# Gate and up projections fed a joined high/low input, later sums of the stick-breaking attention in fp32r for a pair of heads, the second norm's sum behind the first feed-forward block, and the last product in token halves

## What is computed

```
u = rmsnorm(h); q, k, v, u_pool, u_conv = split(u @ w_in)
merged = [rmsnorm(stick_breaking(q,k,v)), rmsnorm(pool(u_pool)), rmsnorm(conv(u_conv))]
h = h + rmsnorm(merged @ w_out)
u = rmsnorm(h); h = h + rmsnorm((silu(u @ w_gate) * (u @ w_up)) @ w_down)
```

## Time and profile before

| | |
|---|---|
| Median of 3 runs | 1150.9 us (1150.71 to 1151.04) |
| The profiled execution | 1150.66 us, span 1148.7 us |
| TensorE busy | 1132.2 us (99% of the span), 8383 matmuls |
| VectorE, ScalarE, GpSimd busy | 672.1, 527.7, 32.2 us |
| HBM traffic | 200.39 MB by DMA, mean 174 GB/s |

### The profile page before, as it was taken

How to read it: one execution, slowest core, us unless ns; L and a number is a source line. 1 busy time by engine, 2 the same in 40 slices (tenths; PEclk the granted TensorE clock), 3 DMA queues, 4 the chain that set the end, 5 groups by cost and what they waited for, 6 DMA issues and landing times.

```text
span 1148.7 us, 21345 instructions
## 1 busy us (share of the span) xinstructions
PE 1132.2 (99%) x8383; PEld 1075.2 (94%) x8383; DVE 672.1 (59%) x787; ACT 527.7 (46%) x642; POOL 32.2 (3%) x45
## 2 busy tenths in 40 slices
PE   9999999999999989999999999999999999999996
PEld 8999999999999989999999999999999888888885
DVE  5599985545556875555556555655565544444543
ACT  6644465755555563433433343334333434343431
POOL 2000101000000220000000000000000000000000
PEclk9999999999999999999999999999999999999999
DMA  7555544434455366665666666565656555555552
GB/s 248 173 168 172 175 129 147 137 115 136 130 181 179 99 200 185 184 186 181 191 188 183 181 184 183 182 187 181 194 172 197 186 199 188 199 188 196 189 195 91
DMA packets 173647, 200.39 MB, mean 174 GB/s; under 512 B 6257, under 2 KB 149825, under 8 KB 173201
## 3 DMA queue, kind: packets, MB, share of 16 engines
q1 hardware_dynamic: 172848, 197.30, 54.7%
q0 software_dynamic: 608, 1.41, 0.4%
q10 hardware_dynamic: 144, 1.05, 0.3%
HBM read 197.63 MB, written 2.10 MB: 174 GB/s over the span
## 4 chain that ended last, share of the span: by engine, by line
PE 96%; DVE 2%; ACT 0%; issue 0%; POOL 0%; POOLq 0%; DVEq 0%; ACTq 0%
PE ps L960 23%; PE ps L962 23%; PE ps L963 23%; PE ps L1280 7%; PE ps L1279 7%; PE ps L1278 7%; PE ps L991 1%; PE ps L1086 1%; PE ps L1074 1%; DVE u L762 1%; DVE arena L875 1%; PE ps L1103 1%; PE ps L1154 1%; DVE xT L882 0%; PE ps L1011 0%
## 5 line engine op out<-in xcount | busy, mean ns | idle before, releaser
L691 DVE TENSOR_TENSOR w_lo<-raw,w_hi 128x1024 fp32r<-128x1024 f32 x368 | 451.8, 1230 | 427.8 <-ACT w_hi L419 427.4
L419 ACT ACTIVATE w_hi<-raw 128x1024 fp32r<-128x1024 f32 x368 | 389.0, 1058 | 500.8 <-PE ps L963 367.2
L960 PE MATMUL ps<-u,w_hi 128*128 128x256 f32 (+1 forms) x1984 | 566.3, 285 | 2.1 <-DVE u L762 1.4
L962 PE MATMUL ps<-u,w_hi 128*128 128x256 f32 (+1 forms) x1984 | 560.6, 283 | 0.0
L963 PE MATMUL ps<-u,w_lo 128*128 128x256 f32 (+1 forms) x1984 | 558.9, 282 | 0.0
L960 PEld LDWEIGHTS ps<-u,w_hi 128*128 128x128 f32 x1984 | 374.1, 189 | 3.3 <-DVE u L762 1.2
L963 PEld LDWEIGHTS ps<-u,w_lo 128*128 128x128 f32 x1984 | 374.4, 189 | 0.0
L962 PEld LDWEIGHTS ps<-u,w_hi 128*128 128x128 f32 x1984 | 373.8, 188 | 0.2
L1278 PE MATMUL ps<-w_hi,ffn 128*128 128x512 f32 x352 | 136.9, 389 | 0.0
L1279 PE MATMUL ps<-w_lo,ffn 128*128 128x512 f32 x352 | 136.9, 389 | 0.0
L1280 PE MATMUL ps<-w_hi,ffn 128*128 128x512 f32 x352 | 136.9, 389 | 0.0
(11 more groups left out here) (167 smaller groups left out, 535.2 us busy)
## 6 DMA issues: line engine op xcount, KB each, us to landing
raw<-in_w_gate SPq DMA_DIRECT2D x88, 512.0 KB, 4.3
raw<-in_w_up SPq DMA_DIRECT2D x88, 512.0 KB, 3.5
raw<-in_w_down SPq DMA_DIRECT2D x88, 512.0 KB, 3.6
raw<-in_w_in SPq DMA_DIRECT2D x72, 512.0 KB, 3.5
raw<-in_w_out SPq DMA_DIRECT2D x32, 512.0 KB, 3.3
arena<-in_x SPq DMA_DIRECT2D x2, 1024.0 KB, 6.1
out<-f_acc SPq DMA_DIRECT2D x3, 512.0 KB, 2.8
side<-in_w_pw POOLq DMA_DIRECT2D x1, 1024.0 KB, 10.8
```

The costliest lines, as they stand in the source:

```text
L419: act.activation(w_hi[:, slot, :], raw[:, slot, :], ACT.Copy).then_inc(hi_done, 1)
L691: dve.tensor_tensor(w_lo[:, slot, :], raw[:, slot, :], hi_view(w_hi[:, slot, :]), ALU.subtract).then_inc(lo_done, 1)
L960: pe.matmul(outs[m], w_hi[:, slot, at], x_hi, start=start and not (one_bank and m), stop=False, skip_group_check=True)
L962: pe.matmul(outs[m], w_hi[:, slot, at], x_lo, start=False, stop=False, skip_group_check=True)
```

## The change

There are four edits.

1. `pairs` takes the place of `products` in the 22 gate and up blocks. w_hi meets x_hi and x_lo in one matmul of 512 columns (2 x 256, the two halves of `u`'s k tile), whose left half of a PSUM bank gets x_hi*w_hi and whose right half x_lo*w_hi. The w_lo matmul of 256 columns adds to the left half. A block now fills two banks for gate (0, 1) and two for up (6, 7). ACT copies the right halves to SBUF (`keep_low`), DVE adds the left halves (`gate_add`, `up_add`), and then scales in SBUF.
2. Attention steps work on both heads of a pair in one instruction of 832 columns. The softplus is rounded on ACT (`softplus_hi`) and its rest taken on DVE (`softplus_lo`), and `later_sums` runs four fp32r products (hi and lo of two heads) with each matrix in place of fp32 ones. The sums stand three steps behind the scores (`SUMS`) in place of two. The last group's pairs stand four steps apart in place of three.
3. The second norm's `column_sums` stands behind the first block, and the gate and up evacuations of that block add first and scale later.
4. In the last column group of w_down the last four chunks are run first for m = 0 and then for m = 1. Square, factor and residual of a half go as soon as that half is done. The residual is cut into two pieces for m = 0 and four for m = 1.

The core of the diff:

```
-            return Q_OUT + 1 + 3 * (h // 2)
+            return Q_OUT + 1 + 4 * (h // 2)
+    SUMS, VALUES = 3, 4
+    OUT_PIECES = [[slice(0, D // 2), slice(D // 2, D)],
+                  [slice(0, D // 2), slice(D // 2, 3 * D // 4), slice(3 * D // 4, 7 * D // 8), slice(7 * D // 8, D)]]
+    LAST = 4
...
+            def softplus_hi(pr):
+                act.wait_ge(sp_done, pr + 1)
+                act.activation(sp_hi, sp, ACT.Copy).then_inc(sp_hi_done, 1)
...
+            def keep_low(i, b, end):
+                act.wait_ge(chunks_used, i * 2 * CK + end)
...
+                act.copy(tmp_ffn[:, 2 * b, :].rearrange("p (a t) -> p a t", a=2),
+                         ps[:, 6 * b:6 * b + 2, SEQ:2 * SEQ]).then_inc(low_kept, 1)
...
+            def masked(pr):
+                dve.wait_ge(z_made, pr + 1)
+                dve.tensor_tensor(zm, ps[:, 5:7, 0:SM], mask2, ALU.add).then_inc(zm_done, 1)
...
+            def softplus_lo(pr):
+                dve.wait_ge(sp_hi_done, pr + 1)
+                dve.tensor_tensor(sp_lo, sp, hi_view(sp_hi), ALU.subtract).then_inc(sp_lo_done, 1)
...
-            def gate_evac(i, end=Q_FFN + CK):
+            def gate_add(i, end=Q_FFN + CK):
                 dve.wait_ge(chunks_used, i * 2 * CK + end)
-                dve.tensor_tensor(halves(tmp_ffn[:, 0, :]), halves(ps[:, 0, :]), both(r2), ALU.mult).then_inc(gs_done, 1)
+                dve.wait_ge(low_kept, 2 * i + 1)
+                dve.tensor_tensor(halves(tmp_ffn[:, 0, :]), ps[:, 0:2, 0:SEQ], halves(tmp_ffn[:, 0, :]),
+                                  ALU.add).then_inc(g_whole, 1)
+            def gate_scale(i):
+                dve.wait_ge(g_whole, i + 1)
+                dve.tensor_tensor(halves(tmp_ffn[:, 0, :]), halves(tmp_ffn[:, 0, :]), both(r2),
+                                  ALU.mult).then_inc(gs_done, 1)
...
+            def pairs(q, slot, kts, fresh, bank, first, last):
+                pe.wait_ge(lo_done, q + 1)
+                for k, kt in enumerate(kts):
...
+                    for m in range(2):
+                        at = slice(k * BLK + m * P, k * BLK + (m + 1) * P)
+                        pe.matmul(ps[:, bank + m, :].rearrange("p (a t) -> p a t", a=2), w_hi[:, slot, at],
+                                  u[:, kt, :, 0:SEQ], start=first and k == 0, stop=False, skip_group_check=True)
+                        mm = pe.matmul(ps[:, bank + m, 0:SEQ], w_lo[:, slot, at], u[:, kt, 0, 0:SEQ], start=False,
+                                       stop=last and k == len(kts) - 1, skip_group_check=True)
...
+                for part in (sp_hi, sp_lo):
+                    for e in range(2):
+                        pe.matmul(ps[:, 5 + e, 0:SM], negtri_r, part[:, e], start=False, stop=False, skip_group_check=True)
...
-                if s == CK - 1:
-                    pe.wait_ge(h2_acc, NOB - 1)
-                    column_sums(ps[:, 7, 0:SEQ], [accy[:, 0, :], accy[:, 1, :]], ss2_made)
+            pe.wait_ge(h2_acc, NOB - 1)
+            pe.wait_ge(rows_kept, 5)
+            column_sums(ps[:, 2, 0:SEQ], [accy[:, 0, :], accy[:, 1, :]], ss2_made)
...
             with pe.Fori(1, NFB) as i:
-                pe.wait_ge(gs_done, i)
+                pe.wait_ge(g_whole, i)
...
+                for m in range(NQ if whole < DCH else 0):
+                    for d in range(whole, DCH):
+                        mm = down_products(n, d, [m])
+                    mm.then_inc(half_made, 1)
```

More of the change, by code:

```diff
@@ L672, in _ @@
                 n, rest = (q - 4 - Q_DOWN) // DCH, (q - 4 - Q_DOWN) % DCH
-                if q - 4 >= Q_DOWN and rest == DCH - 1:
+                if q - 4 >= Q_DOWN and rest == DCH - 1 and n < DN - 1:
                     act.wait_ge(chunks_used, q - 3)
@@ L683, in _ @@
                     act.sem_inc(down_free, 1)
-            act.wait_ge(sst_done, 1)
-            inv_rms(rd, sst, D, rd_done)
+            for m in range(NQ):
+                act.wait_ge(half_made, m + 1)
+                act.wait_ge(dsq_done, NQ * (DN - 1) + m)
+                act.activation(tmp_ffn[:, 0, :], ps[:, 2 + 2 * ((DN - 1) % 2) + m, :], ACT.Square,
+                               accum_out=ssd[:, m, DN - 1:DN]).then_inc(dsq_done, 1)
+                act.wait_ge(sst_done, m + 1)
+                inv_rms(rd[:, m:m + 1], sst[:, m:m + 1], D, rd_done)
         @block.vector
@@ L1253, in ffn_block @@
             def ffn_block(q0, bank):
                 for s in range(CK):
-                    products(q0 + s, s, range(s * CK, (s + 1) * CK), ffn_input, two(bank), s == 0, s == CK - 1, True)
+                    pairs(q0 + s, s, range(s * CK, (s + 1) * CK), False, bank, s == 0, s == CK - 1)
             with pe.Fori(1, NFB) as i:
-                pe.wait_ge(gs_done, i)
+                pe.wait_ge(g_whole, i)
                 ffn_block(i * 2 * CK + Q_FFN, 0)
-                pe.wait_ge(us_done, i)
@@ L1261, in _ @@
-                ffn_block(i * 2 * CK + (Q_FFN + CK), 1)
-            with pe.Fori(0, DN // 2) as i:
-                for b in range(2):
-                    pe.wait_ge(down_free, i * 4 + (2 * b + 2))
-                    for d in range(DCH):
-                        slot = (b * DCH + d) % WSLOTS
-                        pe.wait_ge(lo_done, i * 2 * DCH + (Q_DOWN + b * DCH + d + 1))
-                        pe.wait_ge(f_lo, d + 1)
-                        for k in range(2):
-                            kt = 2 * d + k
-                            mv = slice(k * DCOLS, (k + 1) * DCOLS)
-                            for m in range(NQ):
-                                o = ps[:, 2 + 2 * b + m, :]
-                                rows_m = slice(m * P, (m + 1) * P)
-                                first, last = d == 0 and k == 0, d == DCH - 1 and k == 1
-                                pe.matmul(o, ffn[:, kt, 0, rows_m], w_hi[:, slot, mv], start=first, stop=False)
-                                pe.matmul(o, ffn[:, kt, 0, rows_m], w_lo[:, slot, mv], start=False, stop=False)
-                                mm = pe.matmul(o, ffn[:, kt, 1, rows_m], w_hi[:, slot, mv], start=False, stop=last)
-                        mm.then_inc(chunks_used, 1)
@@ new lines, in _, with down_products @@
+                pe.wait_ge(u_whole, i)
+                ffn_block(i * 2 * CK + (Q_FFN + CK), 6)
+            def down_products(n, d, halves):
+                slot = (n * DCH + d) % WSLOTS
+                pe.wait_ge(lo_done, Q_DOWN + n * DCH + d + 1)
+                pe.wait_ge(f_lo, d + 1)
+                for k in range(2):
+                    kt = 2 * d + k
+                    mv = slice(k * DCOLS, (k + 1) * DCOLS)
+                    for m in halves:
+                        o = ps[:, 2 + 2 * (n % 2) + m, :]
+                        rows_m = slice(m * P, (m + 1) * P)
+                        first, last = d == 0 and k == 0, d == DCH - 1 and k == 1
+                        pe.matmul(o, ffn[:, kt, 0, rows_m], w_hi[:, slot, mv], start=first, stop=False)
+                        pe.matmul(o, ffn[:, kt, 0, rows_m], w_lo[:, slot, mv], start=False, stop=False)
+                        mm = pe.matmul(o, ffn[:, kt, 1, rows_m], w_hi[:, slot, mv], start=False, stop=last)
+                return mm
@@ L1284 @@
+            for n in range(DN):
+                pe.wait_ge(down_free, 2 * n + 2)
+                whole = DCH if n < DN - 1 else DCH - LAST
+                for d in range(whole):
+                    down_products(n, d, range(NQ)).then_inc(chunks_used, 1)
+                for m in range(NQ if whole < DCH else 0):
+                    for d in range(whole, DCH):
+                        mm = down_products(n, d, [m])
+                    mm.then_inc(half_made, 1)
 _INS = ['x', 'meta_tokens', 'pre_mix_g', 'w_in', 'w_pool', 'pool_scale', 'w_dw', 'b_dw', 'conv_ln_g', 'conv_ln_b',
```

249 lines of the change are left out of this document (146 added, 103 removed).

## The result

The changed kernel takes 1139.7 us (median of four runs, 1137.55 to 1140.06). The kernel before took 1150.97 us beside it. The ratio is 0.9894, with a 95% interval of 0.9881 to 0.9906: some 1.1% faster. The forecast of 1131.5 us had the sign right and 8 us too much gain, and the time lies 2.7 us above the range.

The account below looks back on a forecast made before the run. TensorE, busy 99% of the span, was taken to bound the kernel. Savings of 13.8 + 0.6 + 1.2 + 3.8 = 19.4 us gave 1131.5 us against the median of 1150.9, with a range of 1124.5 to 1137.

Parts of the forecast that it names:

- What bounds the kernel: Whole kernel: time is the sum of TensorE's instruction costs; 118.4 ns per 256-column matmul, 226.6 ns per 512-column one.
- Gate and up: Gate and up blocks: joined matmuls cut each of 1408 pieces from 355.2 to 345.0 ns, saving 13.8 us.
- I take the w_down price: Gate and up: the joined 512-column matmul, though two stretches with a gap, costs 226.6 ns as in w_down.
- What the joined form adds: Gate and up: extra PSUM copies and additions, about 1.2 us on ACT and 1.4 on DVE per block, hidden by buffers.
- Later sums: Attention's sums: fp32r products take 2.18 us a pair instead of 2.25, saving 0.6 us for eight pairs.
- first rival: Attention's sums: narrow fp32r matmuls cost only a weight load, saving 4.4 us (7.6 at lowest price); 1127.7 us, chance 0.30.
- I cost this at nothing: Attention: the chain from scores to sums ends with 1.3 us to spare, so no wait of TensorE was counted.
- the pair's chain is late: Rival, attention: chain 2.3 us longer makes TensorE wait 1.0 us at eight pairs, 8 us; 1139.5 us, chance 0.08.
- Second norm: Second norm: TensorE's 2.22 us wait for GpSimd goes, a wait for the split stays; net 1.2 us saved.
- The end: Behind the last matmul: one square less, 2.6 instead of 5.0 us residual, smaller last store; 3.8 us saved.

Follow-up runs that it names:

- e11: Changed kernel with the pair's weights one step earlier on ACT and DVE, and the second half's residual and stores in two pieces; 1136.31 us, ratio 0.9870.
- e9: Changed kernel with w_down's matmuls reading their 512 columns as two stretches of 256, output not the layer's; 1137.0 us, one run.
- e3: Changed kernel with the FFN input in one stretch, without the 16-column gap; 1144.33, 1144.17, 1134.88 and 1135.17 us, ratio 0.9882.
- e7: The same kernel as e3 (FFN input in one stretch) run again; 1135.13, 1135.24, 1135.16 and 1144.38 us, ratio 0.9890.
- e5: Changed kernel with gate and up's w_lo matmul made 512 columns wide too, an extra product no reader needs; 1296.39 us, ratio 1.1265.
- e6: Changed kernel with the two wide matmuls of a chunk's row ahead of the two narrow ones in gate and up; 1141.95 us, ratio 0.9923.
- e10: Changed kernel with gate and up's weights taken from the FFN input instead of the chunk slots, products not the layer's; 1143.07 us, one run.
- e4: Changed kernel with a pair's weights on ACT and DVE moved from behind the second chunk's split to behind the first's; 1136.09 us, ratio 0.9869.
- e12: Changed kernel with early weights and two stores, as in e11, and the FFN input in one stretch; 1133.26 us, ratio 0.9850.

## Why the prediction was right or wrong

**What bounds the kernel: right.** TensorE's own matmuls set the time, and 99% busy at a clock of 1.00 stays true. A window's count gave prices that held: 118.4 ns forecast and 117.5 measured for the narrow matmul beside a wide one, 226.7 in w_down.

**Gate and up, the step that failed.** The text said "I take the w_down price". The mechanism, that most of the overhead goes by the instruction, was right: the piece fell from 355.0 to 348.4 ns. The size was off. The wide matmul costs 230.8 ns in the changed kernel's trace and 232.5 in that of e11, not 226.6. In the traces that makes 8.9 us over 21 blocks where 13.7 was forecast. The median lies 2.1 us above the trace, since three of its four runs are at the upper level. No trace of the changed kernel shows that level; by e11's it is again the price of the piece. Of the 8.2 us by which the median misses the forecast, 4.8 and these 2.1 thus lie in gate and up. The other rows add 0.5 at the second norm, 0.8 at the end and 0.3 at the start, less 0.4 in the attention part. "What the joined form adds" on ACT and DVE is hidden, as forecast: TensorE has no idle time in these blocks.

The Trainium skill's rule for an isolated matmul that the text weighed ("TensorE: Matmul & The Clock Gate", section Back-to-back issue gap) would, as an estimate, have saved 2.5 ns a piece; 6.6 were measured. The rows of this kernel were the better guide, though one of them was read from another stage than the one it priced.

Why the wide matmul is dearer here is **not settled**. The gap between the stretches is not the cause: e9 pays nothing for two stretches, and e3 and e7, without the gap, are once dearer (353.4) and once cheaper (346.7) than with it. A narrow neighbour is not needed for it (e5). Nothing speaks for the change of width (e6) or the weight slots (e10), but with the levels these two runs do not exclude them. What is shown is that the price comes in levels, that a level can change where the stream of pieces is broken and otherwise stays, here through all 21 blocks, and that it accounts for the distance between the profiled runs of e3 and e7. What picks it is open.

**Later sums: the forecast's price was wrong, the first rival's nearly right.** The text took 0.24 us for a 144-column matmul, from the fp32 row of the same width, and 0.12 for a 32-column one. Measured are eight of both in 0.81 us (266.55 to 267.36), 0.10 each. So 5.5 us are saved, between the rival's 4.4 and its lower bound of 7.6. The four of 416 columns took 0.75 us, 0.74 forecast.

**"I cost this at nothing": wrong, in a place that was not looked at.** The chain to the sums was worked out and held nearly: it makes TensorE wait 0.8 us once. The chain from the sums to the values was not worked out. Before the change the two lay two chunks apart, and now one. Behind the sums stand DVE's and ACT's weights: DVE's behind two splits and six taps, ACT's behind a split and DVE's part. TensorE waits 3.1 us for them. e4 takes 2.7 us of that away and gets 1.4 of it back ahead of the sums. The two errors, 4.9 us too little saved and 3.9 us of idle time missed, nearly cancel: 0.6 forecast, 1.0 measured. The rival "the pair's chain is late" gave 1139.5 us, which is the time that came, but by 8 us lost ahead of the sums; there it is 0.8, and the agreement is chance.

**Second norm: right in place, 0.5 us too high.** GpSimd's 2.22 us became 1.17 for the split, and the factor came late by 0.19. The first block's waits for its own splits and input grew from 2.0 to 2.3 us, probably since joined pieces use up chunks faster.

**The end: 3.0 instead of 3.8 us.** The residual went from 5.00 to 2.74 us and one square is gone, as forecast. The last store of 128 KB was priced at 1.9 us, from the first of the five stores of before; behind three others it takes 2.7. That is the missing 0.8.

**The rest.** The first projection matmul started 0.3 us later in the changed kernel. Over the traces of all kernels with this beginning it lies between 18.1 (e9) and 18.7 us (e4), so this is scatter.

## What to carry to other kernels

Where an edit takes a stage of slack out of a software pipeline, work out the chain on both sides of what moved: here the one up to the sums was checked, and TensorE waited 3 us for the one behind them. A price for a matmul holds for the stream it was read in; the same width was 4 to 6 ns dearer in another stage (10 in e3), and 1408 pieces made that the largest error. With differences of 2 ns an instruction, take several runs and more than one trace, since one trace can show either of two levels.

## What was not expected of the hardware

The distance between matmuls in one unbroken stream takes different values for the same code, and keeps its value for hundreds of microseconds: 346.7 or 353.4 ns for a wide and a narrow one in e7 and e3, 348.4 or 350.1 in the changed kernel and e11, always at a granted clock of 1.00 and with TensorE never idle. It can change within one execution where the stream is broken and starts again (353.3, then 346.7 ns in e12). The kernel before has two groups of runs too, some 1.4 us apart; only one trace of it was taken, and what separates them is not known.

fp32r matmuls of 144 and 32 columns cost 0.10 us on average, with 128 columns of weights loaded for each. In fp32 one matmul, which stands as two records in the trace, took 0.24 us with 144 columns and 0.14 with 32. An fp32 value becomes two fp32r parts, so there are twice as many matmuls, and the eight narrow ones of a pair still cost no more than the four in fp32 did (0.81 against 0.77 us). The saving comes from the 416-column ones, 0.75 us for four against 1.48 for two.
